# A latent attention stage rewritten: input by tokens, latents normed there, rope as one product, scores in banks of four or two heads, sums by a column of ones

## Chip, cores and metric

The kernel runs on one core of a Trainium2 chip. The time is device microseconds for one execution. Engines are named as in the profile: PE (TensorE), DVE (VectorE), ACT (ScalarE), POOL (GpSimd), SP (which issues the weight transfers here).

## The reference

Two transformer blocks follow each other, for one sequence of 256 tokens and model width 1024, all in fp32. The first block holds a gated linear attention, a gMLP and a SwiGLU. The second has two layers, each with a SwiGLU, a mixer and another SwiGLU; its first mixer is a stick-breaking attention and its second a latent attention. Only that last mixer is touched:

```python
def multi_head_latent_attention(h, positions, w_in, q_norm, w_uq, kv_norm, w_ukv, w_out):
    proj = h @ w_in
    c_q = proj[..., :MLA_Q_LORA]
    c_kv = proj[..., MLA_Q_LORA:MLA_Q_LORA + MLA_KV_LORA]
    k_rope = apply_rope(proj[..., MLA_Q_LORA + MLA_KV_LORA:][:, :, None, :], positions)[:, :, 0, :]
    q = (rms_norm(c_q, q_norm) @ w_uq).reshape(b, s, MLA_HEADS, MLA_NOPE_DIM + MLA_ROPE_DIM)
    q_nope, q_rope = q[..., :MLA_NOPE_DIM], apply_rope(q[..., MLA_NOPE_DIM:], positions)
    kv = (rms_norm(c_kv, kv_norm) @ w_ukv).reshape(b, s, MLA_HEADS, MLA_NOPE_DIM + MLA_V_DIM)
    k_nope, v = kv[..., :MLA_NOPE_DIM], kv[..., MLA_NOPE_DIM:]
    # per block of 128 queries, causal
    scores = (q_nope . k_nope + q_rope . k_rope) * scale
    o = softmax(scores) @ v
    return o @ w_out
```

There are 16 heads, 256 query latents, 128 key and value latents, 64 + 32 dimensions of a query or key, and 64 of a value.

## The kernel before

The program is one chain of stages. Each stage multiplies a 256-token activation by weights that pass once through SBUF. SP loads weights in the order of `weight_plan()` into ten slots (`RAW`); a slot's next transfer waits for the product that last used it (`used`). Every chunk of weights is split on chip into two fp32r halves: ACT copies the high part (`WH`, L991), DVE subtracts it for the low part (`WL`, L1485). A product in full precision is then three fp32r matmuls (high by high, high by low, low by high). Each engine runs its own list of instructions in the order in which the code writes it, and waits on counters (`sig`, `at`).

Feed-forward stages are written with `lagged`: the first half of the tokens (h = 0) runs four steps ahead of the second. Between stages `boundary(b, c0)` renews the residual `X`, its rms factor and its transposed split form `XH`, `XL`, and splits the first weights of the next stage up to `c0 + 5`.

The latent attention stands between `boundary(5)` and `boundary(6)`:

- Its input product runs dimension-major, for all 256 tokens together (`by_k_step`, L374 to L376), once the last part of `XL` is there. ACT copies it to `CQ`, scales and splits it into `CH`, `CL`; squares are summed over dimensions on PE with a column of ones (L860), and the rms factors are spread by more matmuls (L398).
- Queries come in eight products of two heads, 96 rows each (`q_products`), keys in eight products of two heads whose 128 columns hold keys and values (`k_heads`), values apart (`values`).
- Rope: DVE swaps halves (`rotate`, L2064), multiplies by the sine (L2067), POOL multiplies by the cosine (L2196), DVE adds (L2078), four heads at a time.
- Then a loop over heads. `mla_scores` makes the 384 causal columns of one head and two masks (L923 to L928) in one PSUM bank; DVE takes two maxima and scales them (L2137, L2138, L2141); ACT takes two exponentials with sums (L1458, L1460); DVE divides (L2146 to L2149); PE transposes (L937), ACT copies (L1466), PE multiplies by the values (L949, L950); ACT and DVE split the heads' output (`OH`, `OL`).
- The output product (`mlao_step`, L691) is eight steps for each token half, six matmuls a step. The first half's steps 0 to 5 stand at head 14, near the loop's end; its step 7 after the last head.

## Time and profile before

| | |
|---|---|
| median of 3 runs | 1640.84 us (1639.19 to 1641.54) |
| the profiled execution | 1636.97 us, span 1635.7 us |
| busy over the span | PE 94%, PE weight load 78%, DVE 56%, ACT 48%, POOL 3% |
| mean granted clock of PE | 0.962 |
| last product of the stage before | about 1279.4 us |
| first product of the feed-forward stage after | 1438.57 us |

The profile lists instructions with start and duration. PE instructions overlap at their ends, so what one costs in a row of its kind is the distance of the starts. The windows give busy time in a stretch and PE's granted clock as a share of full speed.

### The profile page before, as it was taken

The page shows a single profiled execution, that of the slowest core. Times are in us where ns is not written, and L with a number is a line of the kernel's source. Part 1 is how long each engine was busy: PE and PEld are TensorE (multiplying, and loading weights), DVE is VectorE, ACT ScalarE, POOL GpSimd, SP SyncE. Part 2 cuts the span into 40 slices and gives each one's busy share as a digit, 9 for nine tenths or more (in the row PEclk, how much of TensorE's full clock was granted, in tenths as well). Part 3 has the DMA queues.
Part 4 walks back from the last instruction along what each step waited for, and adds up shares of the span by engine and source line. Part 5 has one row for each costly group of instructions (what it writes and reads, how often), then busy time and mean ns, then how long its engine had stood idle before and what let it go on. Part 6 is the DMA issues. An engine that isn't in the chain of part 4 may idle for free.

```text
span 1635.7 us, 20070 instructions
## 1 busy us (share of the span) xinstructions
PE 1540.1 (94%) x8188; PEld 1277.9 (78%) x8188; DVE 917.1 (56%) x1294; ACT 792.2 (48%) x1153; POOL 47.8 (3%) x83
## 2 busy tenths in 40 slices
PE   7998999998999999999999999999999777899998
PEld 3897888886888878887898788878888675578886
DVE  2627664877555565555455655556554457365553
ACT  2525435554445355544565555455554444365542
POOL 1000200000000000000021000000000011000000
PEclk9999788999999999999999999999999888799999
DMA  9225353644565655555533455555555410145652
GB/s 380 79 81 204 128 194 129 232 145 163 182 187 186 201 164 186 185 191 180 168 128 126 155 184 184 193 180 179 185 188 190 146 54 26 37 155 183 188 185 103
DMA packets 72236, 267.11 MB, mean 163 GB/s; under 512 B 8016, under 2 KB 8272, under 8 KB 70736
## 3 DMA queue, kind: packets, MB, share of 16 engines
q1 hardware_dynamic: 69984, 258.87, 48.0%
q10 hardware_dynamic: 2160, 6.95, 1.2%
q8 instruction: 65, 1.06, 0.3%
q14 instruction: 27, 0.22, 0.0%
HBM read 264.74 MB, written 1.05 MB: 162 GB/s over the span
## 4 chain that ended last, share of the span: by engine, by line
PE 83%; DVE 8%; ACT 5%; issue 2%; DMA 1%; POOL 0%; ACTq 0%; SPq 0%; DVEq 0%
PE PS L691 20%; PE PS L707 12%; PE PS L709 12%; PE PS L708 12%; PE PS L342 4%; PE PS L343 4%; PE PS L344 4%; DVE WL L1485 2%; ACT WH L991 2%; PE PS L675 1%; PE PS L442 1%; PE PS L374 1%; PE PS L375 1%; PE PS L376 1%; PE PS L563 1%
## 5 line engine op out<-in xcount | busy, mean ns | idle before, releaser
L1485 DVE TENSOR_TENSOR WL<-RAW,WH 128x1024 fp32r<-128x1024 f32 (+1 forms) x472 | 569.9, 1224 | 361.7 <-ACT WH L991 361.2
L991 ACT ACTIVATE WH<-RAW 128x1024 fp32r<-128x1024 f32 (+1 forms) x472 | 484.4, 1053 | 290.6 <-DMA RAW<-in_up 169.9
L707 PE MATMUL PS<-WH,XH 128*128 128x512 f32 x912 | 376.7, 413 | 24.5 <-DVE WL L1485 14.4
L709 PE MATMUL PS<-WH,XL 128*128 128x512 f32 x912 | 357.9, 392 | 0.0
L708 PE MATMUL PS<-WL,XH 128*128 128x512 f32 x912 | 357.7, 392 | 0.0
L707 PEld LDWEIGHTS PS<-WH,XH 128*128 128x128 f32 x912 | 172.2, 189 | 77.3 <-DVE WL L1485 18.3
L709 PEld LDWEIGHTS PS<-WH,XL 128*128 128x128 f32 x912 | 172.0, 189 | 37.0
L708 PEld LDWEIGHTS PS<-WL,XH 128*128 128x128 f32 x912 | 172.6, 189 | 27.7
L691 PE MATMUL PS<-WH,GH 128*128 128x512 f32 x440 | 137.3, 393 | 0.0
L691 PE MATMUL PS<-WL,GH 128*128 128x512 f32 x440 | 135.6, 389 | 0.0
L691 PE MATMUL PS<-WH,GL 128*128 128x512 f32 x440 | 135.6, 389 | 0.0
L691 PEld LDWEIGHTS PS<-WH,GL 128*128 128x128 f32 x440 | 82.6, 188 | 17.4
L691 PEld LDWEIGHTS PS<-WL,GH 128*128 128x128 f32 x440 | 82.6, 188 | 17.4
L691 PEld LDWEIGHTS PS<-WH,GH 128*128 128x128 f32 x440 | 81.2, 188 | 17.2
L1958 DVE SCALAR_TENSOR_TENSOR GG<-PS,RP,SL 128x256 f32<-128x256 f32 x88 | 42.6, 484 | 88.7 <-ACT SL L1291 88.7
L1298 ACT ACTIVATE GH<-PS 128x256 fp32r<-128x256 f32 x110 | 42.2, 384 | 90.9 <-PE PS L675 90.8
L342 PE MATMUL PS<-HH,WH 128*128 128x256 f32 x224 | 66.0, 295 | 0.0
L343 PE MATMUL PS<-HL,WH 128*128 128x256 f32 x224 | 65.3, 292 | 0.0
L344 PE MATMUL PS<-HH,WL 128*128 128x256 f32 x224 | 65.2, 291 | 0.0
L675 PE MATMUL PS<-CST,GG 128*128 128x128 f32 x220 | 58.8, 271 | 0.0
L1291 ACT ACTIVATE SL<-PS,RP 128x256 f32<-128x256 f32 x88 | 41.7, 474 | 28.7 <-PE PS L709 28.7
L342 PEld LDWEIGHTS PS<-HH,WH 128*128 128x128 f32 x224 | 45.1, 201 | 0.9 <-issue 0.3
(365 smaller groups left out, 2133.8 us busy)
## 6 DMA issues: line engine op xcount, KB each, us to landing
RAW<-in_up SPq DMA_DIRECT2D x220, 512.0 KB, 4.7
RAW<-in_down SPq DMA_DIRECT2D x110, 512.0 KB, 3.2
RAW<-in_win SPq DMA_DIRECT2D x44, 512.0 KB, 5.4
RAW<-in_mod SPq DMA_DIRECT2D x32, 512.0 KB, 4.9
MC<-in_mod SPq DMA_DIRECT2D x8, 1024.0 KB, 16.8
RAW<-in_sbqk SPq DMA_DIRECT2D x16, 512.0 KB, 4.8
GROW<-in_grow ACTq DMA_DIRECT2D x9, 512.0 KB, 4.6
RAW<-in_wo SPq DMA_DIRECT2D x8, 512.0 KB, 3.7
```

What stands on the lines that cost most here:

```text
L342: e.matmul(out_, lh, rh, start=first, stop=False)
L343: e.matmul(out_, lh, rl, start=False, stop=False)
L344: return e.matmul(out_, ll, rh, start=False, stop=last)
L675: m = e.transpose(o_[:, y * P:(y + 1) * P], gg[:, y * P:(y + 1) * P], IDN)
L691: m = e.matmul(b2[n][:, :], l, r[:, n * 512:(n + 1) * 512], start=(first and z == 0), stop=(last and z == 2), skip_group_check=True)
L707: e.matmul(o_[:, :], l, w[:, s], start=(k == 0), stop=False, skip_group_check=True)
L708: e.matmul(o_[:, :], l, wl[:, s], start=False, stop=False, skip_group_check=True)
L709: m = e.matmul(o_[:, :], ll, w[:, s], start=False, stop=(k == KD - 1), skip_group_check=True)
L991: e.activation(WH[s][:, 0:c], RAW[s][:, 0:c], ACT.Copy).then_inc(*sig("hi", j))
L1298: e.activation(GH[:, 2 * j:2 * j + 2, h * P:(h + 1) * P], two(BANK.of(("gt", v, j, h))[:, 0:T]), ACT.Copy).then_inc(*sig("gh", v, j, h))
L1485: e.tensor_tensor(WL[s][:, 0:c], RAW[s][:, 0:c], WH[s][:, 0:c].bitcast(F32), ALU.subtract).then_inc(*sig("lo", j))
L1958: m = e.scalar_tensor_tensor(gg[:, :], u, RP[:, v, h:h + 1], sl[:, :], ALU.mult, ALU.mult)
```

## The change

All of it serves the latent attention.

- Input by tokens: `mla_step` multiplies each token half by weights 448 wide (latents, the key's rope part and the same part with halves swapped), first half first, as in the feed-forward stages.
- Latents are normed where tokens are partitions: ACT squares with a sum along the row (`latents`), DVE scales, PE transposes (`latents_turned`), DVE applies the gain, ACT and DVE split.
- Rope as one product: the weights for queries hold for each head 64 plain, 32 rope and 32 swapped rope columns; DVE multiplies the product by a table of ones, cosines and signed sines (`queries`), and the contraction over 128 rows in the scores adds both halves. POOL has no work left here, nor has `rotate`. The table and two fp32r constants for the mask are made in the stage of `ffn(3)`.
- Scores: for the first 128 queries four heads share a bank (128 columns each), for the second 128 two heads (256 columns each). One fp32r matmul masks a bank, one reduction takes its maxima, and the scale is in the keys.
- Sums by a column of ones: values are stored with a 65th column of ones; `mixed` multiplies the transposed weights (as the stationary operand) by 65 columns per head. DVE divides the result instead of the weights; the result is transposed (`mixed_turned`), four blocks in a bank.
- The output product's first token half is spread over the loop, its two banks being held back from the ring (`hold`); all eight steps of the second half follow the loop.

```diff
-            plan += [("mla", i, 1024) for i in range(4)]
-            plan += [("mlaq", i, 768) for i in range(2)]
+            plan += [("mla", i, 2 * MW) for i in range(4)]
             plan += [("mlakv", i, 1024) for i in range(2)]
-            plan += [("mlaq", 2 + i, 768) for i in range(2)]
+            plan += [("mlaq", i, 1024) for i in range(4)]
             plan += [("mlao", i, 1024) for i in range(8)]
         else:
...
+            def mla_step(p, h):
+                pe.wait_ge(*at("xl", 5, h, p // 2))
+                m = narrow(("mp", h), "mla", p, h, ("cn", h, 3), p == 0, p == 3, n=MW)
+                if h or p == 3:
+                    m.then_inc(*sig("mp", p, h))
+                used[chunk["mla", p]] = ("mp", p, 1)
...
+            def keys(h, z):
+
+                w, wl, split = weights("mlakv", 0)
...
+                for y in range(4):
+                    c = slice((4 * z + y) * P, (4 * z + y + 1) * P)
+                    m = three(o_[:, y * P:(y + 1) * P], w[:, c], wl[:, c], CH[:, 2, hs], CL[:, 2, hs], True, True)
+                m.then_inc(*sig("kk", h, z))
+                used[chunk["mlakv", 0]] = ("kk", h, z)
+
...
+                for y in range(2 if h else 4):
+                    x, n = (2 * i + y, T) if h else (4 * i + y, P)
+                    e.matmul(o_[:, y * n:(y + 1) * n], QF[:, x, h * P:(h + 1) * P], KF[:, x, 0:n], start=(y == 0),
+                             stop=False, skip_group_check=True)
+                if h:
+                    masked = o_[:, :].rearrange("p (a b c) -> p a b c", a=2, b=2)[:, :, 1, :]
+                else:
+                    masked = four(o_[:, :])
+                e.matmul(masked, IDNR[:, :], NEGR[:, :].unsqueeze(1).to_broadcast([P, 2 if h else 4, P]), start=False,
+                         stop=True, skip_group_check=True).then_inc(*sig("ms", h, i))
+
+            def weights_turned(h, i):
+                o_, empty = bank(("mt", h, i), ("pt", h, i))
+                px = PX.of(("px", h, i))
+                pe.wait_ge(*at("ex", h, i, 1 if h else 3))
...
-                e.matmul(b[:, 0:128], QF[0:96, h, 0:P], KF[0:96, h, 0:P], start=True, stop=False,
-                         skip_group_check=True)
-                e.matmul(b[:, 128:384], QF[0:96, h, P:T], KF[0:96, h, :], start=False, stop=False,
-                         skip_group_check=True)
-                e.matmul(b[:, 0:128], IDN, NEGM, start=False, stop=False, skip_group_check=True)
-                e.matmul(b[:, 256:384], IDN, NEGM, start=False, stop=True,
-                         skip_group_check=True).then_inc(*sig("ms", h))
-
...
+                first = h == 0 or i % 2 == 0
+                for y in range(2 if h else 4):
+                    x = 2 * i + y if h else 4 * i + y
+                    for t in range(h + 1):
+                        m = e.matmul(o_[:, x % 4 * 65:x % 4 * 65 + 65], pt[:, (y * (h + 1) + t) * P:(y * (h + 1) + t + 1) * P],
+                                     VA[:, t, x * 65:x * 65 + 65], start=(first and y == 0 and t == 0), stop=(t == h),
+                                     skip_group_check=True)
+                m.then_inc(*sig("mo", h, i))
...
-                e.matmul(b[p0:p0 + 64, 0:256], v(0), pt[:, 0:256], start=True, stop=False, skip_group_check=True)
-                e.matmul(b[p0:p0 + 64, 128:256], v(1), pt[:, 256:384], start=False, stop=True,
-                         skip_group_check=True).then_inc(*sig("mbo", h))
-
...
+            for p in range(8):
+                if p < 4:
+                    mla_step(p, 0)
+                if 3 <= p <= 4:
+                    turn(5, 1, p - 3)
+                if p == 7:
+                    latents_turned(0)
+                if p >= 4:
+                    mla_step(p - 4, 1)
+            keys(0, 0)
+            latents_turned(1)
+            keys(0, 1)
+            values(0)
+            keys(1, 0)
+            keys(1, 1)
+            queries(0)
+            values(1)
...
+            scores(1, 3)
+            for i in range(2, 9):
+                if i == 3:
+                    mixed_turned(0, 1)
+                if i == 6:
+                    mixed_turned(1, 0)
+                mlao_step(i - 2, 0)
+                if i == 2:
+                    BANK.hold(("mlao_", 0, 0))
+                    BANK.hold(("mlao_", 0, 1))
+                mixed(1, i - 1)
+                if i < 8:
+                    weights_turned(1, i)
+                if i < 6:
+                    scores(1, i + 2)
             mlao_step(7, 0)
-            for k in range(4, 8):
+            BANK.release(("mlao_", 0, 0))
+            BANK.release(("mlao_", 0, 1))
+            for k in range(8):
...
+                if k == 2:
+                    mixed_turned(1, 1)
                 mlao_step(k, 1)
                 if k >= 6:
                     turn(6, 0, k - 6)
...
+            def weighed(h, i):
+
+                px, before = PX.take(("px", h, i), ("mt", h, i))
+                b, mx = BANK.of(("ms", h, i)), MX.of(("mx", h, i))
+                ac.wait_ge(*at("mx", h, i))
+                ac.wait_ge(*after(before))
+                n = T if h else P
+                for y in range(2 if h else 4):
+                    s = slice(y * n, (y + 1) * n)
+                    e.activation(px[:, s], b[:, s], ACT.Exp, bias=mx[:, y:y + 1],
+                                 scale=1.0).then_inc(*sig("ex", h, i, y))
...
-                    dv.wait_ge(*at("rcp", x))
-                    e.tensor_scalar(sx[:, 0:128], sx[:, 0:128], mx[:, 6:7], None, ALU.mult).then_inc(*sig("dvd", x, 0))
-                    e.tensor_scalar(sx[:, 128:384], sx[:, 128:384], mx[:, 7:8], None,
-                                    ALU.mult).then_inc(*sig("dvd", x, 1))
...
+            def queries(x):
+                dv.wait_ge(*at("mq", x))
+                dv.wait_ge(*at("dve", "tab"))
+                e.tensor_tensor(QF[:, 2 * x:2 * x + 2, :], two(BANK.of(("mq", x))[:, :]), TAB[:, :, :],
+                                ALU.mult).then_inc(*sig("qf", x))
...
+            for i in range(2, 9):
+                if i == 3:
+                    mixed_turned(0, 1)
+                if i == 6:
+                    mixed_turned(1, 0)
+                if i % 2 == 0:
+                    mixed(1, i // 2 - 1)
+                if i < 6:
+                    greatest(1, i + 2)
+                if i < 8:
+                    mlao_split(i)
+            mixed_turned(1, 1)
             boundary(6, chunk["up", UP * FFN[6]])
...
-            for x in range(5):
-                n = 4 if x else 1
-                dst = QF[R4, 4 * x - 4:4 * x, :] if x else CQ[R4, 3:4, :]
-                po.wait_ge(*at("shf", x))
-                po.wait_ge(*at("act", "cos"))
-                e.tensor_tensor(dst, dst, COS[R4, :].unsqueeze(1).to_broadcast([32, n, T]),
-                                ALU.mult).then_inc(*sig("rcs", x))
 
```

PE, one turn of the loop. Before, head 9 and the first products of head 10 (`KF<-`/`KF,QF`: scores; `SX`: weights to be transposed; `VT`: values):

```order
L923 MATMUL PS<-KF,QF 128x128
L925 MATMUL PS<-KF,QF 128x256
L927 MATMUL PS<-CST 128x128
L928 MATMUL PS<-CST 128x128
L937 MATMUL PS<-CST,SX_209 128x128 x3
L949 MATMUL PS<-PT_214,VT 64x256
L950 MATMUL PS<-PT_214,VT 64x128
```

Now, one turn for two heads (`MOH`, `MOL`: the split input of the output product; `VA`: values with ones; `PX`: weights to be transposed):

```order
L722 MATMUL PS<-WH_91,MOH 128x512 x2
L722 MATMUL PS<-WL_81,MOH 128x512 x2
L722 MATMUL PS<-WH_91,MOL 128x512 x2
L986 MATMUL PS<-VA,PT_217 128x65 x4
L969 MATMUL PS<-CST,PX_207 128x128 x4
L954 MATMUL PS<-KF,QF 128x256 x2
L960 MATMUL PS<-NEGR,IDNR 128x2x128
```

A step of the output product now stands in each turn; before, all of them stood behind the loop or at its last heads.

DVE, from the end of the loop into `boundary(6)`. Before (`OL`: heads' low part; `Y`, `X`: residual; `WL`: low part of weights; `TN`: first step towards the next `XL`):

```order
L2023 TENSOR_TENSOR OL<-PS,OH 128x256 x2
L1857 TENSOR_TENSOR Y_106<-PS,GROW_61 128x512
L1857 TENSOR_TENSOR Y_107<-PS,GROW_61 128x512
L1870 TENSOR_TENSOR STA<-STA 128x1
L1874 RECIPROCAL STA<-STA 128x1
L1890 SCALAR_TENSOR_TENSOR X<-Y_107,STA,X 128x512
L1890 SCALAR_TENSOR_TENSOR X<-Y_106,STA,X 128x512
L1485 TENSOR_TENSOR WL_78<-RAW_68,WH_88 128x1024
L1485 TENSOR_TENSOR WL_79<-RAW_69,WH_89 128x1024
L1902 TENSOR_TENSOR TN_163<-PS,SM 128x512
```

Now:

```order
L2277 TENSOR_TENSOR MOL<-PS,MOH 128x4x128
L1999 TENSOR_TENSOR Y_106<-PS,GROW_61 128x512
L1999 TENSOR_TENSOR Y_107<-PS,GROW_61 128x512
L2012 TENSOR_TENSOR STA<-STA 128x1
L2016 RECIPROCAL STA<-STA 128x1
L2032 SCALAR_TENSOR_TENSOR X<-Y_107,STA,X 128x512
L2032 SCALAR_TENSOR_TENSOR X<-Y_106,STA,X 128x512
L1627 TENSOR_TENSOR WL_76<-RAW_66,WH_86 128x1024
L1627 TENSOR_TENSOR WL_77<-RAW_67,WH_87 128x1024
L1627 TENSOR_TENSOR WL_78<-RAW_68,WH_88 128x1024
L1627 TENSOR_TENSOR WL_79<-RAW_69,WH_89 128x1024
L2044 TENSOR_TENSOR TN_163<-PS,SM 128x512
```

Two splits of the next stage's weights that stood in the loop now stand ahead of `TN`.

## Rows read from the trace of the kernel before

**Rows 1.** Windows: busy time of each engine in stretches, PE's granted clock, DMA.

```profile
1200.00:1277.60 77.60, 77.60 (x350) 63.77 (x349) 40.23 (x45) 36.01 (x45) 0.00 (x0) 1.00 0.57 187
...
1337.00:1375.40 38.40, 26.02 (x147) 20.83 (x148) 29.37 (x67) 19.34 (x52) 6.78 (x2) 0.83 0.10 35
1375.40:1410.20 34.80, 24.47 (x100) 15.98 (x98) 20.47 (x57) 19.62 (x52) 0.00 (x0) 0.70 0.00 1
1410.20:1438.57 28.37, 26.78 (x117) 21.06 (x116) 7.60 (x13) 8.26 (x15) 0.00 (x0) 0.95 0.39 121
```

**Rows 2.** Waits of PE from 1277 to 1439: total us, times, longest.

```profile
PE PS L937 <- DVE SX L2149: 19.2, 9, 5.8
PE PS L860 <- ACT SQM L1409: 4.7, 1, 4.7
PE PS L665 <- DVE X L1890: 4.5, 1, 4.5
```

**Rows 3.** The chain that ended last, 1200 to 1440: start, duration, what.

```profile
1323.22 3.42 POOL QF L2196
...
1392.49 0.28 DVE MX L2137
...
1398.06 0.55 ACT SX L1458 x2
...
1401.65 0.28 DVE MX L2137
```

**Rows 4.** Timeline of PE, fp32r matmuls of 256 and of 512 columns.

```profile
1295.08 0.28 PE L376 MATMUL PS<-XH,WL 128*128 128x256 f32 x1
1295.20 0.28 PE L374 MATMUL PS<-XH,WH 128*128 128x256 f32 x1
...
1430.46 0.62 PE L691 MATMUL PS<-WH,OH 128*128 128x512 f32 x2
1430.92 0.62 PE L691 MATMUL PS<-WL,OH 128*128 128x512 f32 x2
```

**Rows 5.** Timeline of PE, one head of the loop with no wait.

```profile
1348.77 0.60 PE L925 MATMUL PS<-KF,QF 96*128 96x256 f32 x2
1349.21 0.39 PE L927 MATMUL PS<-CST 128*128 128x128 f32 x2
...
1349.65 0.49 PE L937 MATMUL PS<-CST,SX 128*128 128x128 f32 x3
1350.07 0.65 PE L949 MATMUL PS<-PT,VT 128*64 128x256 f32 x2
1350.56 0.38 PE L950 MATMUL PS<-PT,VT 128*64 128x128 f32 x2
1350.87 0.36 PE L342 MATMUL PS<-CH,WH 128*96 128x256 f32 x1
```

**Rows 6.** Timeline of PE in the first block, fp32 matmuls of 64 columns.

```profile
186.09 0.43 PE L563 MATMUL PS<-QI,S 128*128 128x64 f32 x2
186.45 0.43 PE L561 MATMUL PS<-SC,VTX 64*128 64x64 f32 x2
```

**Rows 7.** Groups by line, 1287.8 to 1430.66: busy, mean ns, idle before.

```profile
L1466 ACT ACTIVATE PT<-PS 128x384 f32<-128x384 f32 x16 | 7.8, 486 | 12.4 <-PE PS L937 12.2
...
L2138 DVE TENSOR_REDUCE MX<-PS 128x1 f32<-128x256 f32 x16 | 6.6, 414 | 0.0
```

**Rows 8.** Timeline of DVE in `boundary(6)`.

```profile
1430.66 1.41 DVE L1857 TENSOR_TENSOR Y<-PS,GROW 128x512 f32<-128x512 f32 x2 [4.87 <-PE PS L691]
...
1434.16 2.36 DVE L1485 TENSOR_TENSOR WL<-RAW,WH 128x1024 fp32r<-128x1024 f32 x2
```

**Rows 9.** Timeline of DVE and of PE at both ends of the stage.

```profile
1279.62 0.69 DVE L1913 TENSOR_TENSOR XL<-TN,XH 128x512 fp32r<-128x512 f32 x1 [0.70 <-ACT XH L1247]
...
1284.56 1.97 PE L665 MATMUL PS<-CST,X 128*128 128x128 f32 x8 [4.54 <-DVE X L1890]
...
1438.57 0.50 PE L707 MATMUL PS<-WH,XH 128*128 128x512 f32 x1 [1.59 <-DVE XL L1913]
```

More of the change, by code:

```diff
@@ L693, in wide, with narrow @@
                 return m
-            def narrow(name, kind, i, h, free, first, last, between=None):
+            def narrow(name, kind, i, h, free, first, last, between=None, n=512):
                 w, wl, split = weights(kind, i)
@@ new lines, in values @@
+            def values(h):
+                w, wl, split = weights("mlakv", 1)
+                hs = slice(h * P, (h + 1) * P)
+                pe.wait_ge(*split)
+                pe.wait_ge(*at("cl", h))
+                for n in range(2):
+                    o_, empty = bank(("vl", h, n), ("dve" if n else "act", "vl", h))
+                    c = slice(n * 512, (n + 1) * 512)
+                    pe.wait_ge(*empty)
+                    three(o_[:, :], CH[:, 2, hs], CL[:, 2, hs], w[:, c], wl[:, c], True,
+                          True).then_inc(*sig("vl", h, n))
+                used[chunk["mlakv", 1]] = ("vl", h, 1)
@@ new lines, in dve_program @@
+            latents(0)
+            split(chunk["mlaq", 0])
+            latents_gained(0)
+            latents_low(0)
+            latents(1)
+            latents_gained(1)
+            latents_low(1)
+            values_kept_of(0, 1)
+            split(chunk["mlaq", 1])
+            values_kept_of(1, 1)
+            for x in range(2):
+                queries(x)
+            split(chunk["mlaq", 2])
+            queries(2)
+            queries(3)
+            greatest(0, 0)
+            split(chunk["mlaq", 3])
```

623 lines of the change are left out of this document (328 added, 295 removed).

## Prediction

> **What bounds the kernel now.** Over the whole span PE is the bound: in a feed-forward stretch it is busy in all of 77.60 us at full clock, while DVE has 40.23 and ACT 36.01 [rows 1]. The latent attention is the exception, so I read windows by stage first. In its loop over heads PE is busy 26.02 of 38.40 and 24.47 of 34.80 us, and those at a granted clock of 0.83 and 0.70, a mix of 2.4 and 1.2 GHz [rows 1]. The waits say for what: PE waited 19.2 us for DVE's division of the weights, 4.7 us once for the squares of the latents, and 4.5 us once for the residual at the start [rows 2]. The chain of waits shows the loop as a serial circuit of DVE, ACT and DVE again: from 1392.49 to 1401.65 it makes two heads, 4.58 us a head [rows 3]. PE's own work for a head, counted where nothing waited, is 2.3 us: .44 for the 256-column score, .22 each for the 128-column score and two masks, .42 for three transposes, .49 and .31 for the values [rows 5]. So half of a head's time is latency. Ahead of the loop, rope hangs on POOL, 3.42 us for four heads [rows 3]. The output product then stands almost whole behind the loop, 28.37 us to the next stage [rows 1].
>
> The stretch that the change can move runs from 1280.3, when the first `XL` is ready (1279.62 + 0.69), to 1438.57, the next stage's first product [rows 9]: 158.3 us. I work out that stretch anew; all before and behind it I take as unmoved.
>
> **PE's work in the new stage.** Distances of starts at full clock: fp32r 256 columns .12 and 512 columns .227 (two in .455) [rows 4]; fp32 128 columns .22 (two masks in .44) and 256 columns .44; a transpose .14 with a change of kind in it, .12 without; a change from one kind of product to the next costs .09 (L950 takes .31 for 128 columns, not .22) [rows 5].
>
> - Input: 48 of 448 columns, .227 x 448/512 = .20: 9.5.
> - Keys: 48 of 128 columns in fp32r, a size that the trace doesn't show. Below it lies nothing cheaper than half of .12, above it fp32's .22. I take .12, the nearest row of fp32r: 5.8 (2.9 to 10.6).
> - Values 12 of 512: 2.7. Queries 96 of 256: 11.5.
> - Scores 16 of 128 and 16 of 256 columns in fp32, 3.5 + 7.0; masks 4 of 512 and 8 of 256 in fp32r, 1.9: 12.4. Before, the masks alone were 32 fp32 matmuls at .22.
> - Transposes: 8 of latents, 48 of weights, 16 of outputs, 72 x .12 = 8.6.
> - `mixed`: 48 fp32 matmuls of 65 columns behind a fresh 128 x 128 stationary operand. By columns alone it would be half of .22; the masks, fresh operands too, cost .22; the 64-column products of the first block cost .36 [rows 6], but they change the shape of the array's tile each time, which `mixed` doesn't. I take .22: 10.6 (5.3 to 17.3).
> - Output product 96 x .227 = 21.8. Four turns of `X`: 1.8.
>
> Sum 84.7. About 45 changes of kind at .09 add 4.0.
>
> The trace has no 128-column fp32r row. The Trainium skill, TensorE: Matmul & The Clock Gate, section Back-to-back issue gap, puts a sustained stream of weight load and 128-column matmul at about 81 ns; by that figure the keys would be 3.9 in place of 5.8 and the stage 1.9 us shorter, an estimate from the page. The same page, section LDWEIGHTS, speaks against `mixed`: a load takes the number of its columns over 1.2, 107 ns for 128, and this change makes the 128-wide weights the stationary side where 64-wide values stood. An fp32 matmul shows two loads here, so by the page 48 x .213 = 10.2, not the 5.3 by columns; no row before has just that shape.
>
> **Waits that remain for PE.**
>
> - Start. Steps 0 to 3 of the first token half fill the 4.5 us in which PE waited [rows 2], 4.8 us from 1280.3. Then come both turns; before, 3.3 us lay between the start of the turns and the first product behind them (1284.56 to 1287.85, which is ACT and DVE at work), of which the turns are .9. With no product left in between I keep a wait of 2.3.
> - Latents. The norm now waits for the boundary's last rms factor, then ACT squares and takes a root, DVE makes four small operations, PE transposes, DVE, ACT, DVE finish, for each half. One such chain cost 4.7 before [rows 2]. The two halves cover each other in part, the key and value products stand between: 5 (0 to 9.4).
> - The last query weights are split on DVE behind the first maximum: maximum of 512 columns, about .7 (256 cost .414 [rows 7], and I add .14 for each 128), then a split 1.2 (two in 2.36 [rows 8]), against no PE work: 1.5 after the overlap.
> - Loop. A turn for two heads on PE is 1.36 (product) + .9 (`mixed`) + .5 (transposes) + 1.1 (scores, mask) = 3.9 with changes of kind. ACT in a turn: copy .5 (384 columns cost .486 [rows 7]), two exponentials of 256 without their sums .9, a split 1.0: 2.4. DVE: maximum .7, split 1.2, half of a division .6: 2.2. Scores are issued two banks ahead, so PE should not wait; I allow 1.0 in all.
> - End. Behind step 7 of the first half PE has eight steps of the second (10.9), four transposes of outputs (.5) and two turns (.9): 12.3. DVE first needs those transposes (two steps and .5 in, 3.2), ACT's copy and its own subtraction (1.4), the residual as before, 3.5 from `Y` to the splits [rows 8], then four splits where two stood, 4.8, and `TN`, `XH`, `XL` at .7 each [rows 9]: 14.9. PE waits 2.6. Here 2.4 us are given back, since the splits that the loop's last heads used to make are not in the new loop. Weights are no limit: the third and fourth chunks of the next stage wait for slots that the first two steps of the second half free, and the queue moves a chunk in under 5 us, before DVE gets to them.
>
> Waits: 2.3 + 5 + 1.5 + 1 + 2.6 = 12.4.
>
> **Clock.** With gaps of 2 to 3 us in the first 20, part of PE's early work will run at 1.2 GHz, as the loop did at 0.70 and 0.83 with gaps. I count 7 us of work at twice the time: 3.5 (0 to 12).
>
> **What I cost at nothing.** The tables in the stage of `ffn(3)` are six short DVE operations for one, and two ACT copies, some 2 us; DVE is idle in half of such a stretch [rows 1]. If that cover is gone, they cost 2. Transfers: input weights shrink by 4 x 128 columns and query weights grow by 4 x 256, 0.26 MB more in all, with DMA at a share of 0.00 to 0.10 in the loop. POOL's and the shuffle's work goes away and had stood on the path, but my sum is of the new path, so nothing is subtracted for them.
>
> **Sum.** 84.7 + 4.0 + 12.4 + 3.5 = 104.6 us for what took 158.3: 53.7 less. The profiled execution took 1636.97 (span 1635.7), so it would be 1583.3. The median of the runs shown lies 3.9 above it, 1640.84, so the time is 1587.1. Of the 104.6, 84.7 are PE at full clock, which leaves little room for a much larger gain.
>
> **Rivals.**
>
> - *The prices at the upper bounds.* Keys at .22 and `mixed` at .36 add 4.8 + 6.7 = 11.5: gain 42, 1598.6. For it speak rows 6, against it that masks with fresh operands cost .22. Chance 0.12.
> - *Still a serial circuit.* If a bank's scores, maximum, exponentials, transposes, copy and `mixed` follow each other with the product between, a turn is 1.1 + .7 + .9 + .5 + .5 + .9 + 1.36 and some .3 of hops, 6.3 in place of 3.9; seven turns are 17, the first four banks some 5 more: gain 32, 1609. That is what the old loop is; against it stands the written order, with scores two banks ahead. Chance 0.16.
> - *Slower.* PE stays at 1.2 GHz through the stage, as it did for much of the old loop, because of waits that I have counted too small. All 88.7 us of work cost as much again, less the 3.5 already counted: 85.2 more, 1672.3. It turns from gain to loss when 57.2 of the 88.7, 64% of the work, runs at 1.2 GHz. For it speaks the clock of 0.70; against it 0.95 once the output product runs [rows 1], which now stands in each turn. Chance 0.02.
> - *Better.* The latents' wait hides and the clock holds: 5 + 3.5 less, gain 62, 1578.6. Chance 0.06.
> - *Nothing happens.* Only if the whole gain went into a wait I don't see; 0.01 for within 0.2%, which is about what a measurement tells from no change.
>
> **How the numbers follow.** The forecast has 0.63, with a range of its own of 1580 to 1595. To leave out no more than 2 in 10 the range takes in the better case's larger part, the upper prices and the near half of the serial case: 1577 to 1604. Faster by over 0.2% is everything but the slower rival and unseen mishaps: 0.96; within 0.2% 0.01; slower 0.03.
>
> **What the new profile would show.** The next stage's first product near 1384.9 instead of 1438.57. PE's waits for DVE in the loop under 2 us in sum; turns 3.9 us apart. `mixed` matmuls .22 apart, keys .12. One PE wait of 2 to 3 us for `XL` ahead of the next stage, with four splits before `TN` on DVE. Two waits around the latents of together 5. Clock at 1.00 in the loop. I would be wrong if DVE or ACT, not PE, were busy without a break in the loop, or if the clock stayed below 0.9 there.

## The result and the profile after

The changed kernel takes 1587.38 us (median of 4 runs, 1583.72 to 1589.56), the kernel before 1640.26 (4 runs, 1639.19 to 1641.54): ratio 0.9675, 95% interval 0.9653 to 0.9697, 52.9 us less. The forecast was 1587.1, 53.7 less. The profiled execution took 1583.72 (span 1582.1).

The stage, from the first product of the latent attention's input to the next stage's first product, in the timeline of PE of the changed kernel, in answer to [rows 9]:

```profile
1283.68 0.47 PE L738 MATMUL PS<-WH,XH 128*128 128x448 f32 x1
...
1385.04 0.50 PE L738 MATMUL PS<-WH,XH 128*128 128x512 f32 x1 [2.86 <-DVE XL L2055]
```

It lasts 101.4 us, where I had 104.6 and the old one took 158.3. Behind it nothing moved: 1582.1 - 1385.04 = 197.06, before 1635.7 - 1438.57 = 197.13. But it starts 3.4 us later than the 1280.3 of before, so the span's gain of 53.6 is 56.9 in the stage, less those 3.4, and 0.1 behind.

The same stage in windows (columns as in [rows 1]; the number ahead of the DMA share is PE's granted clock):

```profile
1283.68:1298.00 14.32, 9.93 (x50) 8.63 (x50) 10.78 (x27) 8.89 (x20) 0.00 (x0) 1.00 0.46 147
1298.00:1302.00 4.00, 3.98 (x16) 3.42 (x17) 2.13 (x3) 1.46 (x6) 0.00 (x0) 0.57 0.60 243
1302.00:1306.00 4.00, 2.98 (x24) 2.83 (x23) 2.00 (x7) 3.74 (x9) 0.00 (x0) 0.89 0.50 135
1306.00:1310.00 4.00, 4.00 (x21) 3.47 (x20) 1.55 (x3) 3.71 (x6) 0.00 (x0) 0.69 0.00 0
1310.00:1340.00 30.00, 28.00 (x222) 26.80 (x220) 16.93 (x27) 18.75 (x40) 0.00 (x0) 1.00 0.32 106
1340.00:1368.00 28.00, 26.45 (x171) 23.30 (x170) 15.21 (x23) 16.70 (x28) 0.00 (x0) 1.00 0.00 1
1368.00:1385.04 17.04, 13.95 (x66) 11.34 (x66) 10.21 (x17) 9.39 (x15) 0.00 (x0) 1.00 0.68 229
```

PE is busy 89.28 of 101.36 us, at full clock but for 12 us in front; in the loop (1340 to 1368) 26.45 of 28, where it had been busy 26.02 of 38.40 at 0.83 [rows 1]. The same windows over the whole old stage give PE 119.17 us busy of 158.27. Taking busy time times one minus the clock as what the clock cost, old and new split so:

| us | before | after | gain |
|---|---|---|---|
| PE idle | 39.1 | 12.1 | 27.0 |
| lost to the clock | 19.3 | 3.3 | 16.0 |
| work at full clock | 99.9 | 86.0 | 13.9 |

Three quarters of the gain are waits and clock; the work itself shrank by a seventh. By place, 12.9 of the 56.9 us lie ahead of the first score matmul (47.7 before, from 1280.3 to 1328.0, and 34.8 now), the rest behind it. The waits of PE, 1283 to 1390, in answer to [rows 2] (total us, times, longest):

```profile
PE PS L738 <- DVE XL L2055: 4.6, 2, 2.9
PE PS L900 <- DVE CN L2226: 3.7, 2, 2.7
PE PS L722 <- DVE WL L1627: 1.8, 3, 0.7
PE PS L373 <- DVE WL L1627: 1.6, 1, 1.6
PE PS L986 <- ACT PT L1555: 0.4, 1, 0.4
```

DVE's division, 19.2 us before, is gone, and no wait of that size took its place: in the loop there are 1.8 us for `WL` and 0.4 for `PT`.

One turn of the loop in the timeline of PE, in answer to [rows 5]:

```profile
1342.52 0.63 PE L722 MATMUL PS<-WH,MOH 128*128 128x512 f32 x2
...
1343.91 1.00 PE L986 MATMUL PS<-VA,PT 128*128 128x65 f32 x8
1344.75 0.61 PE L969 MATMUL PS<-CST,PX 128*128 128x128 f32 x4
1345.20 1.03 PE L954 MATMUL PS<-KF,QF 128*128 128x256 f32 x4
1345.88 0.47 PE L960 MATMUL PS<-NEGR,IDNR 128*128 128x256 f32 x1
1346.18 0.60 PE L996 MATMUL PS<-CST,OT 128*128 128x128 f32 x4
1346.54 0.71 PE L722 MATMUL PS<-WH,MOH 128*128 128x512 f32 x2
```

By the distances of the starts: product 1.39, four `mixed` matmuls .84, four transposes .45, two scores and the mask .98, the extra transposes of outputs .36: 4.02 us for two heads. The next turn, without the last item, takes 3.74, the three behind it 4.20, 4.23 and 3.67. One head took 4.58 [rows 3].

### The profile page after: what moved, and what is told of

Its sections match the earlier page's. It is cut to its first block, busy times and chain, and to the rows that moved or that the text cites. A ratio compares the mean times of both kernels' runs of the same rounds, so it can differ in the third digit from the quotient of the medians.

```text
span 1582.1 us, 19799 instructions
## 1 busy us (share of the span) xinstructions
PE 1515.6 (96%) x8114; PEld 1264.2 (80%) x8114; DVE 893.7 (56%) x1217; ACT 785.4 (50%) x1121; POOL 27.3 (2%) x78
## 4 chain that ended last, share of the span: by engine, by line
PE 86%; DVE 7%; ACT 4%; issue 1%; DMA 1%; ACTq 0%; SPq 0%; POOL 0%; DVEq 0%
PE PS L722 21%; PE PS L738 13%; PE PS L740 13%; PE PS L739 13%; PE PS L373 4%; PE PS L374 4%; PE PS L375 4%; DVE WL L1627 2%; PE PS L706 2%; ACT WH L1082 1%; PE PS L473 1%; PE PS L594 1%; PE PS L592 1%; PE PS L405 1%; PE PS L406 1%
## 5 line engine op out<-in xcount | busy, mean ns | idle before, releaser
L1627 DVE TENSOR_TENSOR WL<-RAW,WH 128x1024 fp32r<-128x1024 f32 x472 | 568.3, 1220 | 347.9 <-ACT WH L1082 347.4
L1082 ACT ACTIVATE WH<-RAW 128x1024 fp32r<-128x1024 f32 x472 | 483.7, 1054 | 289.4 <-DMA RAW<-in_up 169.7
L738 PE MATMUL PS<-WH,XH 128*128 128x512 f32 (+1 forms) x928 | 384.8, 415 | 26.7 <-DVE WL L1627 13.6
L740 PE MATMUL PS<-WH,XL 128*128 128x512 f32 (+1 forms) x928 | 365.5, 394 | 0.0
L739 PE MATMUL PS<-WL,XH 128*128 128x512 f32 (+1 forms) x928 | 365.0, 393 | 0.0
L738 PEld LDWEIGHTS PS<-WH,XH 128*128 128x128 f32 x928 | 176.1, 190 | 80.3 <-DVE XL L2055 17.2
L740 PEld LDWEIGHTS PS<-WH,XL 128*128 128x128 f32 x928 | 176.0, 190 | 37.4
L739 PEld LDWEIGHTS PS<-WL,XH 128*128 128x128 f32 x928 | 176.9, 191 | 28.2
```

What stands on the lines that cost most here:

```text
L738: e.matmul(o_[:, 0:n], l, w[:, s], start=(k == 0), stop=False, skip_group_check=True)
L739: e.matmul(o_[:, 0:n], l, wl[:, s], start=False, stop=False, skip_group_check=True)
L740: m = e.matmul(o_[:, 0:n], ll, w[:, s], start=False, stop=(k == KD - 1), skip_group_check=True)
L1082: e.activation(WH[s][:, 0:c], RAW[s][:, 0:c], ACT.Copy).then_inc(*sig("hi", j))
L1627: e.tensor_tensor(WL[s][:, 0:c], RAW[s][:, 0:c], WH[s][:, 0:c].bitcast(F32), ALU.subtract).then_inc(*sig("lo", j))
```

## Experiments

PE's instructions ahead of the stage are the same in all of these kernels, and yet the stage starts between 1281.2 and 1286.7. So beside the times I compare two pieces of the profiled execution: the *head*, from the stage's first product to the first score matmul, and the *tail*, from there to the next stage's first product. All figures in us; the ratio is to the kernel before, measured in the same session.

| kernel | head | tail | median | ratio (95% interval) |
|---|---|---|---|---|
| changed kernel | 34.8 | 66.5 | 1587.38 | 0.9675 (0.9653 to 0.9697) |
| early_splits | 34.9 | 64.3 | 1580.04 | 0.9641 (0.9620 to 0.9661) |
| early_end | 35.0 | 64.1 | 1578.80 | 0.9636 (0.9621 to 0.9650) |
| no_spread | 33.2 | 74.8 | 1591.59 | 0.9721 (0.9697 to 0.9744) |
| one_ahead | 34.9 | 91.6 | 1610.88 | 0.9828 (0.9810 to 0.9846) |
| splits_first | 34.9 | 68.1 | 1587.63 | 0.9684 (0.9654 to 0.9713) |
| masks_fp32 | 39.8 | 70.3 | 1583.95 | 0.9681 (0.9656 to 0.9706) |
| divided | 36.6 | 71.6 | 1592.64 | 0.9707 (0.9682 to 0.9732) |
| latents_first | 34.6 | 66.6 | 1584.27 | 0.9669 (0.9655 to 0.9683) |
| wide_keys | 33.9 | 66.5 | 1584.80 | 0.9672 (0.9656 to 0.9688) |
| filler | 32.7 | 66.6 | 1582.63 | 0.9656 (0.9642 to 0.9671) |
| combined2 | 29.6 | 64.5 | 1575.14 | 0.9611 (0.9595 to 0.9627) |
| combined3 | 29.6 | 62.5 | 1573.51 | 0.9604 (0.9591 to 0.9618) |

### What the written order is worth

**no_spread**

```diff
-                mlao_step(i - 2, 0)
...
-            mlao_step(7, 0)
...
+            for k in range(8):
+                mlao_step(k, 0)
             for k in range(8):
```

(The two banks are not held back here.)

> The eight output-product steps of the first token half stand together behind the loop instead of one in each turn; nothing else is changed. Theory A, the spreading is what hides the latency: ACT and DVE need about 4 us for a turn (maximum 0.7, two exponentials 0.84, a split 1.0 and 1.2, copy 0.6, hops), so the turn stays near 4 us, PE waits about 1.4 us in each, and the product's 7 steps of 1.4 us come behind: +8 to +11 us, with a granted clock below 1.00 in the loop on top. Theory B, the shorter chain alone is what counts: with scores two banks ahead PE sets the turn also without the product, the turn shrinks from 4.0 to about 2.7 us, and the time rises by 0 to 2 us.

The tail is 8.3 us longer, 4.9 of it PE's idle time and 3.1 its work at half clock; the head, in which nothing was changed, was 1.6 us shorter by its clock. `mixed` now waits for ACT's copy in each turn (timeline of PE):

```profile
1346.96 1.11 PE L986 MATMUL PS<-VA,PT 128*128 128x65 f32 x8 [0.84 <-ACT PT L1550]
1350.75 1.11 PE L986 MATMUL PS<-VA,PT 128*128 128x65 f32 x8 [1.26 <-ACT PT L1550]
1354.97 1.11 PE L986 MATMUL PS<-VA,PT 128*128 128x65 f32 x8 [1.25 <-ACT PT L1550]
```

The turns take 3.79 and 4.22 us, although PE has a third less to do. That is theory A: DVE and ACT need about 4 us for two heads, and the product is free there. They do not need it by their work: from 1347 to 1355.6, two turns, DVE is busy 4.9 and ACT 4.5 us. They wait for each other. The maxima stand as far apart as in the changed kernel, where they start at 1346.38, 1350.67, 1354.89 and 1358.57 (timeline of DVE, here):

```profile
1347.70 0.68 DVE L2256 TENSOR_REDUCE MX<-PS 128x2 f32<-128x512 f32 x1
1351.93 0.68 DVE L2256 TENSOR_REDUCE MX<-PS 128x2 f32<-128x512 f32 x1
1355.61 0.68 DVE L2256 TENSOR_REDUCE MX<-PS 128x2 f32<-128x512 f32 x1
```

4.23 and 3.68 here, 4.22 and 3.68 there. So what paces both loops does not run through PE's product; the chain under splits_first shows it. The clock from 1355 to 1370 fell to 0.77.

**one_ahead**

```diff
-            scores(1, 3)
             for i in range(2, 9):
...
-                if i < 6:
-                    scores(1, i + 2)
+                if i < 7:
+                    scores(1, i + 1)
```

(The held banks are also released two steps later, without which PE and DVE would wait for each other.)

> In the loop the scores of a bank are issued one bank ahead instead of two. Theory A, the lead is what keeps it from being a serial circuit: ACT's exponentials and the split then stand between a turn's start and the copy that mixed needs, about 3.2 us where PE has 1.4 us of product, so a turn grows from 4.0 to about 5.5 us and six turns cost +9 us (6 to 11). Theory B, the output product alone covers the latency: +0 to +2 us.

25.0 us longer, far above either. The direction is theory A's, its mechanism is not: PE waited 15.6 us for `WL` in the loop, and only 0.7 for `PT`. The timeline of PE, then those of DVE and ACT:

```profile
1347.59 0.47 PE L960 MATMUL PS<-NEGR,IDNR 128*128 128x256 f32 x1
1351.92 1.22 PE L722 MATMUL PS<-WH,MOH 128*128 128x512 f32 x2 [3.86 <-DVE WL L1627]
...
1362.36 1.22 PE L722 MATMUL PS<-WH,MOH 128*128 128x512 f32 x2 [3.86 <-DVE WL L1627]
```

```profile
1348.10 0.69 DVE L2261 TENSOR_REDUCE MX<-PS 128x2 f32<-128x512 f32 x1 [3.43 <-PE PS L960]
1350.64 1.23 DVE L1627 TENSOR_TENSOR WL<-RAW,WH 128x1024 fp32r<-128x1024 f32 x1 [1.85 <-ACT WH L1082]
```

```profile
1348.82 0.84 ACT L1548 ACTIVATE PX<-PS,MX 128x256 f32<-128x256 f32 x2 [3.35 <-DVE MX L2261]
1349.55 1.05 ACT L1082 ACTIVATE WH<-RAW 128x1024 fp32r<-128x1024 f32 x1
```

Mask, maximum, exponentials, `WH`, `WL`, product, and behind the product the next scores: the split of a weight that has nothing to do with the scores stands behind their exponentials in two lists, and so closes a circuit. Three turns are 10.3 to 10.4 us each, and with these waits the clock was 0.72 from 1340 to 1389. In the turn shown 4.33 us lie between mask and product; the 6.11 from product to mask took 3.36 in the changed kernel, at full clock (1342.52 to 1345.88). In the whole tail 14.2 of the 25.0 us are idle time of PE and 11.0 work at half clock. In my expectation the product needed nothing.

**splits_first.** The changed kernel's loop has a circuit too, but a shorter one, of DVE and ACT alone. Its chain of waits (start, duration, what):

```profile
1354.89 0.69 DVE MX L2261
...
1355.98 0.47 ACT PX L1548
1356.45 0.95 ACT WH L1082
...
1357.43 0.04 DVE WL L1627
1357.46 1.11 issue
1358.57 0.69 DVE MX L2261
...
1362.38 0.74 PE PS L722 x2
```

The exponentials `PX` wait for the maximum `MX`; the split's `WH` stands behind them in ACT's list; `WL` waits for `WH`; and the next maximum stands behind `WL` in DVE's list, though its scores were masked 0.3 to 0.9 us before. That is 3.68 us from maximum to maximum, and 4.2 to 4.3 in turns in which DVE also divides or splits `MOL`. The chain from 1346.4 to 1362.4 is this circuit, so for four turns not PE but DVE and ACT together set the pace, though only just: PE is busy 14.9 of the 16 us, DVE 8.6 and ACT 10.6.

```diff
                 weights_turned(1, i)
+                mlao_split(i)
                 if i < 6:
                     weighed(1, i + 2)
-                mlao_split(i)
```

and the same on DVE, ahead of `greatest`.

> In the loop ACT and DVE split the output product's weights ahead of the exponentials and maxima of their turn instead of behind them. Theory, from the experiment with scores one bank ahead (10.4 us a turn): the remaining waits of the loop come from a circuit scores, maximum 0.7, exponentials 0.84, copy of the high half 1.05, low half 1.23, product, scores, because the split stands behind the exponentials in both lists. Ahead of them it hangs on nothing: PE's three waits for WL (1.8 us in sum) go, the stage is 1.5 to 2 us shorter. Rival: the exponentials, one microsecond later, make the transposes or mixed late instead: 0, or up to 3 us longer.

From the first product of the loop to the fifth it took 15.4 us instead of 16.2, with no wait for `WL` among them. Then `PT` was late (0.8 us), `WL` still late twice at the end (1.0 us), and the clock fell to 0.89 between 1360 and 1375; the tail is 1.5 us longer. The gain at first is what the theory said, the late `PT` is the rival; it did not last. Nor does the split hang on nothing in the new order: on ACT it stands behind the copy `PT`, that behind the exponentials, and on DVE the next maximum stands behind `WL`. The circuit is turned, not opened: its chain has maxima at 1351.17, 1355.83, 1359.99 and 1364.16, 4.2 to 4.7 us apart. PE's idle time in the tail is the same (6.7 and 6.6 us), and 1.7 us are work at half clock; that fall is in this one profile only, so I leave open whether the order is worse or the same. The time says 0.9684, no gain.

### What single parts are worth

**divided**

```diff
-                    e.activation(px[:, s], b[:, s], ACT.Exp, bias=mx[:, y:y + 1],
-                                 scale=1.0)
+                    e.activation(px[:, s], b[:, s], ACT.Exp, bias=mx[:, y:y + 1], scale=1.0,
+                                 accum_out=mx[:, 4 + y:5 + y])
...
+            def divided(h, i):
...
+                e.reciprocal(mx[:, 4:4 + n], mx[:, 4:4 + n]).then_inc(*sig("rcp", h, i))
...
+                e.tensor_tensor(v, v, bc(mx[:, 4:4 + n], 512 // n), ALU.mult).then_inc(*sig("dvd", h, i))
```

> One part undone: ACT sums the exponentials again (a read of the accumulator behind each of 32, about 0.19 us) and DVE divides the 128x512 weights ahead of the transposes (about 0.7 us and a reciprocal a bank), as the kernel before did; the column of ones stays, its sum is then 1. Theory A, order is what took the gain's larger part: with scores two banks ahead the chain has 8 us, a longer chain of 1.3 us is covered and only the waits for the split that stands behind it grow: stage +2 to +5 us. Theory B, the column of ones carries it: DVE and ACT, at 2.2 and 2.4 us of work in a turn of 4.0, get 0.9 and 0.4 more and the circuit of scores, maximum, exponentials, division, split, product is longer than two turns: +8 us or more, with a clock below 1.00 in the loop.

Tail +5.1, at the edge of theory A. By the starts of the products, 4.1 of it lie ahead of the loop (first score to first product 28.16 instead of 24.02), where PE waited four times, 3.3 us, for the divided weights; from the first product to the eighth it took 26.63 instead of 25.71. So a division that had cost 19.2 us of waiting costs 5.1 in all with this order, and in the loop proper 0.9. The head's 1.8 us are nearly all its clock (0.86 for 0.90), with no instruction changed in it.

**masks_fp32**

```diff
-                e.matmul(masked, IDNR[:, :], NEGR[:, :].unsqueeze(1).to_broadcast([P, 2 if h else 4, P]), start=False,
+                e.matmul(masked, IDN, NEGM.unsqueeze(1).to_broadcast([P, 2 if h else 4, P]), start=False,
```

> The twelve mask matmuls take their two constants in fp32 instead of fp32r. Theory A, PE sets the pace from the first scores to the end of the loop: 4 of 512 columns cost 0.87 instead of 0.23 to 0.30, 8 of 256 columns cost 0.43 instead of 0.12 to 0.30, so +3.5 to +5 us. Theory B, in the loop a circuit of DVE and ACT sets the pace: then the eight later ones are hidden in part, +2 to +3 us or less.

Tail +3.8, theory A's lower end. A mask of 512 columns costs .86 where it was .31, one of 256 .44 where it was .30; that is 3.3, and with the two scores ahead of a mask (.86 where they took .68) about 5. PE's smaller idle time gives 0.8 back. The times, 1582.7 to 1595.6 in six runs, are too wide to show it, and their median is even below the changed kernel's: in the profiled one the head alone was 5.0 us longer, at a clock of 0.79, with no instruction changed in it.

### The end of the stage

**early_splits**, on ACT and the same on DVE:

```diff
                 mlao_split(i)
+            mlao_split(9)
             mixed_turned(1, 1)
```

> The first two weights of the next feed-forward stage are split on ACT and DVE right behind the last split of the output product's weights, instead of in the boundary ahead of TN. My theory of the stage's end: PE's last wait, 2.9 us for XL, is four splits on DVE (4.62 us) ahead of TN. Two of them now fall where DVE and ACT had nothing to do (4.99 and 6.17 us of idle time), so TN comes 2.4 us earlier, the wait falls to about 0.5 us and the time by 2.4 us, ratio 0.9985. Rival: the wait is ACT's, which loads a table (1.28 us) and squares ahead of the residual: then the start of X does not move and with two splits fewer behind it the gain is still seen, but less than 1.5 us, because the second half's squares are late next. Rival: raw weights arrive late, no gain.

Timeline of DVE:

```profile
1366.16 2.35 DVE L1628 TENSOR_TENSOR WL<-RAW,WH 128x1024 fp32r<-128x1024 f32 x2
...
1375.91 2.35 DVE L1628 TENSOR_TENSOR WL<-RAW,WH 128x1024 fp32r<-128x1024 f32 x2
...
1379.56 0.69 DVE L2056 TENSOR_TENSOR XL<-TN,XH 128x512 fp32r<-128x512 f32 x1 [0.70 <-ACT XH L1338]
```

PE's last wait fell from 2.86 to 0.6, the tail by 2.3: as expected.

**early_end**, on ACT (DVE as in early_splits):

```diff
-            mixed_turned(1, 1)
+            mlao_split(9)
             e.preload_act_table_set("sqrt_and_others")
+            mixed_turned(1, 1)
```

> The run early_splits with, besides, ACT's table load and its two splits ahead of the copy of the last transposed outputs. What is left of PE's wait in front of the next stage there is 1.0 to 1.2 us; the load (1.28 us) stands between MOH and the squares of the boundary, on which the second Y waits 0.71 us. Theory: the boundary starts about 0.7 us earlier and the wait falls to 0.5 us or less, so the stage is 3.0 us shorter than the changed kernel's (101.4 us), against 2.3 in early_splits. Rival: DVE's own two Y, X, splits and TN set the end, and the load is hidden beside them: 2.3 us as in early_splits.

0.2 us more, the rival by its number but not by its reason: `TN` now waits for PE's own turn of `X` (0.19 us), so it is no longer DVE's list that sets the end, and PE's last wait is 0.34 us.

### The head, and the clock

**latents_first**

```diff
-                if p == 7:
-                    latents_turned(0)
                 if p >= 4:
                     mla_step(p - 4, 1)
+            latents_turned(0)
+            latents_turned(1)
             keys(0, 0)
-            latents_turned(1)
```

with `latents(1)` ahead of `latents_turned(0)` on ACT and of `latents_low(0)` on DVE.

> The transposes of the first half's latents stand behind the whole input product, and ACT and DVE norm the second half's latents before they finish the first. The stage's first two waits are 2.7 and 1.0 us for CN; theory: the second half's chain no longer hangs on the wait for the first one's, both together are done by about 1303.5 instead of 1306.4, and the end of the keys moves by 2 us, less what the weights' split, now later, takes back at the queries: 1 to 3 us shorter. Rival: DVE sets the pace from there to the first scores (four splits, eight products with the table), so the stage does not get shorter and the wait for the last query weights (1.6 us) grows by the same amount.

The head is 0.2 us shorter, which the theory did not expect; nor did the last query weights come later, as the rival had it. Its windows:

```profile
1298.00:1302.00 4.00, 1.35 (x10) 1.04 (x10) 2.97 (x10) 1.34 (x6) 0.00 (x0) 1.00 0.92 289
1302.00:1306.00 4.00, 4.00 (x21) 4.00 (x20) 1.11 (x2) 3.33 (x6) 0.00 (x0) 0.50 0.40 155
1306.00:1310.00 4.00, 4.00 (x19) 3.51 (x19) 1.82 (x2) 3.92 (x6) 0.00 (x0) 0.65 0.00 0
```

The waits were over by 1301.3, and then PE worked without a break, but at 1.2 GHz to 1306 (0.50) and for part of the next 4 us (0.65). The wait for the last query weights was the same 1.56 us. The order itself won little: the two waits for `CN` are 3.3 us where they were 3.7, since the first half's keys no longer stand between them. The clock took what it takes in the changed kernel too, 3.4 us in either head.

**wide_keys**

```diff
-                for y in range(4):
-                    c = slice((4 * z + y) * P, (4 * z + y + 1) * P)
-                    m = three(o_[:, y * P:(y + 1) * P], w[:, c], wl[:, c], CH[:, 2, hs], CL[:, 2, hs], True, True)
+                for y in range(2):
+                    c = slice((2 * u + y) * P, (2 * u + y + 1) * P)
+                    m = three(o_[:, y * T:(y + 1) * T], w[:, c], wl[:, c], CH[:, 2, :], CL[:, 2, :], True, True)
```

in four banks, behind `latents_turned(1)` and `values(0)`.

> Keys for all 256 tokens in one product: 24 fp32r matmuls of 256 columns instead of 48 of 128. The traces so far show 0.112 us for 128 columns and 0.12 for 256, so PE's work is 2.5 us less, but it can start only when both halves' latents are there, and the first half's keys no longer fill that wait. Theory: PE's waits ahead of the keys grow by 0.5 to 1.5 us and the stage gets 1 to 2 us shorter. Rival: all of the saved work turns into waiting, for the second half's latents or at the last query weights: 0.

Head -0.9: PE is busy 26.8 us in it instead of 29.4, and waits 1.7 us more for `CN`. Most of the saved work turned into waiting. The price that made it worth trying is in the changed kernel's timeline of PE, keys above, queries below:

```profile
1311.09 0.27 PE L374 MATMUL PS<-CL,WH 128*128 128x128 f32 x1
1311.20 0.28 PE L375 MATMUL PS<-CH,WL 128*128 128x128 f32 x1
...
1311.72 0.28 PE L373 MATMUL PS<-CH,WH 128*128 128x256 f32 x1
1311.84 0.28 PE L374 MATMUL PS<-CL,WH 128*128 128x256 f32 x1
```

**filler**

```diff
+            FILL = (10, 4)
+            def fill(o_, n):
...
+                for _ in range(n):
+                    e.matmul(four(o_[:, :]), IDNR[:, :], IDNR[:, :].unsqueeze(1).to_broadcast([P, 4, P]), start=True,
+                             stop=True, skip_group_check=True)
...
+                if h == 1 and p == 0:
...
+                    fill(o_, 6)
+                    e.matmul(o_[:, 0:P], IDNR[:, :], IDNR[:, :], start=True, stop=True).then_inc(*sig("fill"))
...
+                fill(o_, FILL[h])
```

> Twenty-one fp32r matmuls whose result nobody reads stand where PE waits at the start of the stage: 7 in front of the second half's first input product, 10 and 4 in front of the two transposes of the latents, 0.23 us each at full clock, so about as long as the waits of 1.7, 2.7 and 1.0 us. They shorten no wait. Theory: the granted clock, 0.57 from 1298 to 1302 and 0.69 from 1306 to 1310 in the changed kernel, fell because PE had stood still; with PE at work through the waits it stays near 1.00, and the first 30 us of the stage, 3.3 us of which are that loss (clock 0.89), get 2 to 3.3 us shorter: stage 98 to 99.5 instead of 101.4. Rival: the clock is taken away for other reasons, the fillers only stand in the way: clock 0.89 as before and the stage 0 to 1 us longer.

```profile
1295.00:1299.00 4.00, 2.52 (x15) 1.73 (x13) 2.88 (x6) 1.93 (x8) 0.00 (x0) 1.00 0.90 293
1299.00:1303.00 4.00, 4.00 (x33) 3.78 (x33) 1.87 (x6) 3.35 (x7) 0.00 (x0) 1.00 0.38 128
1303.00:1307.00 4.00, 4.00 (x31) 3.74 (x31) 2.38 (x3) 3.92 (x7) 0.00 (x0) 1.00 0.00 0
```

The clock is 1.00 in every window of the head, and the head is 2.2 us shorter with 21 matmuls more in it; 1.1 us of the 3.3 came back as a new wait ahead of the keys, which PE now reached sooner. The changed kernel and the seven other kernels with the same head all lost clock in it (0.79 to 0.95), and the three with fillers (this one, combined2 and combined3) did not (1.00). The useful work is the same and in the same order (only the ring of PSUM banks stands one further), so it is the standstill that brought the clock down. Of the 2.2 us, 3.4 are clock; PE's idle time and the fillers together take 1.2 more than its idle time did.

**combined2** holds the edits of wide_keys, latents_first, early_end and filler together, with `FILL = (6, 8)` (and on ACT one weight split between the latents of the two halves, not behind both):

> The edits that pointed to less time together: keys for 256 tokens at once, both halves' latents normed behind the whole input product, fillers in the three waits, the next stage's first two splits early with the table load in front. By their stages, each against 101.4: early splits 2.3, wide keys 1.0, of the latents' order and the fillers 2 to 5 if the clock holds: stage 93 to 96 us, time 5 to 8 us below the changed kernel's. Rival: what is saved at the keys comes back as a longer wait for the last query weights, whose splits stand at fixed places in the lists of ACT and DVE: stage 97 to 98.

Head -5.2, tail -2.1. The stage is 94.1 us, inside the range expected. Of the head's 5.2, 3.4 are the clock, which is 1.00 throughout, and about 2.1 PE's shorter useful work; idle time and fillers together are about 5.8 us where 5.4 were idle. What the latents' order gives in it is not shown: no run has these edits without it.

**combined3**, on DVE, and the same move on ACT:

```diff
             split(chunk["mlaq", 2])
+            split(chunk["mlaq", 3])
             queries(2)
             queries(3)
             greatest(0, 0)
-            split(chunk["mlaq", 3])
```

> The run combined2 with the last query weights split right behind the ones before them, on ACT ahead of the values' copy and the spread of rope, on DVE ahead of two products with the table and the first maximum. Theory: PE's wait of 1.9 us there is a matter of place in two lists; raw weights are there and DVE has 1.3 us of idle time just ahead. The wait falls to 0.5 us or less and the stage from 94.1 to 92.6. Rival: the first maximum, 1.2 us later, makes exponentials and the first transposes late: the wait moves to the transposes of the first bank, the stage stays at 94.

Tail -1.9 more, no wait at the query weights. Its waits, 1283 to 1376:

```profile
PE PS L722 <- DVE WL L1637: 1.7, 3, 0.7
PE PS L738 <- DVE XL L2065: 0.6, 2, 0.3
PE PS L373 <- DVE CL L2251: 0.5, 1, 0.5
...
```

The stage is 92.1 us instead of 101.4. At 1573.51 us it is faster than both kernels: 0.9604 of the one before, and the changed kernel's interval (0.9653 to 0.9697) lies above its own.

Not undone in any run: the input by tokens, the norm of the latents by tokens, rope as one product, and the banks of four and two heads. What each of these is worth is not shown.

## Why the prediction was right

Term by term, for the stage:

| term | predicted | measured |
|---|---|---|
| start wait | 2.3 | 1.7 |
| latents | 5 (0 to 9.4) | 3.7 |
| last query weights | 1.5 | 1.6 |
| loop | 1.0 | 2.2 |
| end | 2.6 | 2.9 |
| clock | 3.5 (0 to 12) | 3.3 |
| work and changes of kind | 88.7 | 86.0 |
| ahead of the stage | 0 | 3.4 |

- *Waits.* 12.1 in all, I had 12.4. The end is the term with the best proof: I wrote that 2.4 us are given back by four splits ahead of `TN`, and early_splits got 2.3 of them. The other four are each within 1.3 us.
- *Loop.* Turn predicted 3.9, measured 3.7 to 4.2; waits predicted 1.0, measured 2.2. The number is near, and the reason is not: I had PE set the pace, with DVE and ACT at 2.2 and 2.4 us of work in a turn. By work that is not far off (8.6 and 10.6 us in four turns), but their instructions stand behind each other in two lists, and this circuit takes 3.7 to 4.3 us (maxima 4.29, 4.22 and 3.68 apart), on most turns more than PE's 3.7 to 4.0. That it is so near PE's own time is luck. no_spread shows it alone, with the same distances of the maxima, and in the changed kernel the profile's chain runs through it for four turns. My sign of being wrong, DVE or ACT busy without a break, would have missed it: neither is. "Scores are issued two banks ahead, so PE should not wait" holds for the longer circuit, through the product, that one_ahead shows (10.4 us a turn, some of it slow clock). The rival *still a serial circuit* was priced by another chain (through transposes and `mixed`) at 6.3; the ones that exist run through the weight split.
- *Prices.* Keys .11 (I took .12, bounds half of it and .22), `mixed` .21 (.22), transposes .11 (.12). The sum is 2.7 too high, part of it the changes of kind: scores and mask of a bank take .98 with their change in it, I had 1.00 and the changes apart. Keys took 112 ns each in a row of 24, not the 81 ns that the Trainium skill, TensorE: Matmul & The Clock Gate, section Back-to-back issue gap, gives for a stream of load and 128-column matmul. The same page, section LDWEIGHTS, puts a load of 128 columns at 107 ns; two of them would be .21, an estimate from the page. The trace agrees: a `mixed` matmul, which moves 65 columns only, takes .21.
- *Clock.* 3.3 for 3.5, and its cause, gaps early in the stage, is shown by filler. The size has luck in it: among eight heads with the same instructions the loss was 1.7 to 8.5 us.
- *Ahead of the stage.* "All before and behind taken as unmoved" is where I was 3.4 us off, and it cancels the 3.2 of the stage: the profiled gain came out right partly by luck. It is not the work that the change adds there, the tables: the groups of turns of `X`, before and after (first and last start), and the table of the changed kernel:

```profile
L665 PE MATMUL PS<-CST,X x80: 270/272/474, 570.4 to 1286.1; 128*128 128x128 f32 x80
```

```profile
L696 PE MATMUL PS<-CST,X x80: 270/272/273, 573.3 to 1289.4; 128*128 128x128 f32 x80
```

```profile
L2148 DVE MEMSET TAB<- x2: 272/272/272, 1049.5 to 1050.5; 64x256 f32 x2
```

At the first of these turns 2.9 of the 3.4 us are there already, more than 470 us ahead of the tables. And from a turn at 902.35 before and 905.59 after to the first `XL` it is 378.0 us in both, so costing the tables at nothing stands.

Of the 3.4, 1.4 are there by 352 us, at the first product of `MH`; there the thirteen profiles of kernels with the same front lie between 349.7 and 355.1, so this part differs from run to run. The other 2.0 are there in all thirteen alike (1.9 to 2.3 more than before's from that product to the first `XL`). They come with the clock: from 365 us to the stage the profile before has one stretch of 3.4 us at half clock, at 587, and the thirteen have three, for instance at 397, 783 and 913 in the changed kernel's. The waits of 1.8 to 2.5 us just ahead of each of the four stand in both kernels. Why they brought the clock down in one and not in the other stays open, and with a single profile of the kernel before no run shows whether it is chance or comes with the change.

## What to carry to other kernels

Where one engine is to stay busy, do not only sum the other engines' work: ask of every instruction in their lists what it stands behind. A weight split behind an exponential, and a maximum behind the split, made a circuit of things that don't depend on each other: 3.7 to 4.3 us a turn, with DVE busy 8.6 and ACT 10.6 of 16 us. Putting an instruction elsewhere in a list opens such a circuit only if nothing on its new place waits for it again (splits_first). Independent work of the bound engine is worth most inside a latency-bound loop (8.3 us here, 4.9 in waits and 3.1 in clock). A wait at the start of a stage costs twice, once as waiting and once as slow work behind it; filling it with useless work won 2.2 us here, where an edit that only shortened it won 0.2.

## What the runs showed of the hardware

- An fp32r matmul of 128 columns costs .112 us and one of 256 .12, with a fresh 128 x 128 stationary operand each time: half the columns save nearly nothing.
- An fp32 matmul of 65 columns behind a fresh 128 x 128 operand costs .21 us, one of 128 columns .22: here too fewer columns save nothing.
- PE's clock falls behind a wait, while PE is already at work again: after waits that ended at 1301.3 it ran at 0.50 from 1302 to 1306, fully busy. 21 matmuls without a use (some 5 us of work) in three waits of 5.4 us kept it at 1.00 and made the stage 2.1 us shorter.
- With nothing changed ahead of it, the same point of the program lies 5.5 us apart between profiles (1281.2 to 1286.7), nearly all of it from the first 352 us (349.7 to 355.1 there), and a head without an edit took 33.2 to 39.8 us at clocks of 0.95 to 0.79: differences of some us need pieces of the trace, not the median alone.
